# The low part of each weight slot, made by GpSimd in four operations of 512 columns in place of one of 2048

## What is computed

```python
def token_mix(x, pool_prev, mem_k, mem_v, pos0, w_in, b_in, ...):
    proj = x @ w_in + b_in                       # u, v, p, q, and three gates
    z = jax.nn.gelu(proj[..., :OFF_P])
    ...
    br_a = (u * mixed.reshape(N, L, A_WIDTH)) @ w_a_out
    p_ext = jnp.concatenate([pool_prev.astype(p.dtype), p], axis=1)
    br_b = pool_mix(p_ext, pos0, w_pool, ls_pool) @ w_b_out
    o = mem_attend(q..., mem_k.astype(q.dtype), mem_v.astype(q.dtype))
    br_m = o.reshape(N, L, MEM_WIDTH) @ w_m_out
    h = gates[:, :, 0] * br_a + gates[:, :, 1] * br_b + gates[:, :, 2] * br_m
    return h @ w_o, p_ext[:, -POOL_HIST:], v
...
y_p = layer_norm(DN_ALPHA * y_p + t_p, ln1_g[l], ln1_b[l])
f_p = moe_ffn(y_p.reshape(-1, D_MODEL), w_r[l], b_r[l], w1[l], b1[l], w2[l], b2[l])   # top 4 of 32 experts
y_p = layer_norm(DN_ALPHA * y_p + f_p, ln2_g[l], ln2_b[l])
```

## Time and profile before

| | |
|---|---|
| Time, median of 3 runs | 1342.45 us (1342.22 to 1343.2) |
| Time of the profiled execution | 1345.13 us |
| Its span, first to last instruction | 1343.3 us |
| TensorE busy (matmul) | 1278.1 us, 95% |
| VectorE busy | 421.4 us, 31% |
| ScalarE busy | 248.2 us, 18% |
| GpSimd busy | 222.4 us, 17%; of it L525: 39 operations, 183.5 us |
| Mean granted TensorE clock | 0.973 of full |
| The chain that ended last | TensorE 75%, DMA 16%, VectorE 4%, ScalarE 2%, GpSimd 1% |

### The profile page before, as it was taken

The page is one execution under the profiler, slowest core; times in us unless marked ns, Lnnn a source line. Parts: engine busy times, 40 slices in busy tenths (PEclk is TensorE's granted clock), DMA queues, the critical chain, the costliest instruction groups (busy, mean ns, idle before and its releaser), DMA issues.

```text
span 1343.3 us, 15957 instructions
## 1 busy us (share of the span) xinstructions
PE 1278.1 (95%) x6440; PEld 663.3 (49%) x6440; DVE 421.4 (31%) x783; ACT 248.2 (18%) x360; POOL 222.4 (17%) x99
## 2 busy tenths in 40 slices
PE   7999999998979999999999999999999999999994
PEld 7989889998843333333333333333333333333331
DVE  3670482284631313212222221312222131222225
ACT  3424443333230111101101010110101011010111
POOL 5536167665420000000000000000000000000001
PEclk9979999998959999999999999999999999999997
DMA  9534675741569999999999999999999999999991
GB/s 315 183 105 164 216 236 179 217 145 44 195 260 429 428 428 429 427 429 427 429 429 429 427 429 428 428 428 428 429 429 428 428 428 427 429 428 428 429 401 40
DMA packets 77179, 464.82 MB, mean 346 GB/s; under 512 B 5553, under 2 KB 44005, under 8 KB 52464
## 3 DMA queue, kind: packets, MB, share of 16 engines
q1 hardware_dynamic: 75616, 459.18, 83.5%
q0 software_dynamic: 1456, 5.11, 1.2%
q10 hardware_dynamic: 72, 0.03, 0.0%
HBM read 461.51 MB, written 2.90 MB: 346 GB/s over the span
## 4 chain that ended last, share of the span: by engine, by line
PE 75%; DMA 16%; DVE 4%; ACT 2%; issue 1%; POOL 1%; SPq 0%; ACTq 0%; DVEq 0%; POOLq 0%
PE ps L1619 27%; DMA big<-in_w 16%; PE ps L1298 15%; PE ps L1662 12%; PE ps L1592 6%; PE ps L1280 4%; PE ps L1309 2%; PE ps L1573 2%; PE ps L1644 1%; PE ps L1391 1%; ACT actT L775 1%; PE ps L1400 1%; POOL ring_lo L525 1%; PE ps L1377 1%; DVE hT_lo L1071 1%
## 5 line engine op out<-in xcount | busy, mean ns | idle before, releaser
L1619 PE MATMUL ps<-big,xg 128*64 128x512 f32 x2048 | 464.4, 597 | 11.4 <-DMA big<-in_w 11.1
L1619 PEld LDWEIGHTS ps<-big,xg 128*64 128x64 f32 x2048 | 139.9, 137 | 301.6 <-issue 264.1
L525 POOL TENSOR_TENSOR ring_lo<-ring,w_hi 128x2048 fp32r<-128x2048 f32 x39 | 183.5, 4708 | 125.2 <-ACT w_hi L606 125.1
L1662 PE MATMUL ps<-big,actT 128*64 128x512 f32 x768 | 171.9, 596 | 3.9
L571 POOL TENSOR_TENSOR yacc<-yacc,ln 128x512 f32<-128x512 f32 x2 | 3.3, 1642 | 949.8 <-ACT yacc L628 949.8
L770 ACT ACTIVATE sg<-gm 128x512 f32<-128x512 f32 x32 | 20.2, 631 | 541.5 <-DVE gm L1202 541.5
L1202 DVE TENSOR_SCALAR gm<-ps 128x512 f32<-128x512 f32 x32 | 22.1, 692 | 312.6 <-PE ps L1619 312.6
L1181 DVE TENSOR_TENSOR yacc<-ps,yacc 128x512 f32<-128x512 f32 (+1 forms) x90 | 61.9, 687 | 144.6 <-PE ps L1592 143.2
L1662 PEld LDWEIGHTS ps<-big,actT 128*64 128x64 f32 x768 | 52.3, 137 | 110.7 <-issue 91.4
L1174 DVE COPY ypair<-ps 64x512 f32<-64x512 f32 x32 | 22.2, 694 | 253.9 <-PE ps L1662 253.9
L1592 PE MATMUL ps<-ypair,pickT 128*128 128x512 f32 (+1 forms) x180 | 96.5, 631 | 0.0
(11 more groups left out here) (276 smaller groups left out, 1155.4 us busy)
## 6 DMA issues: line engine op xcount, KB each, us to landing
big<-in_w SPq DMA_DIRECT2D x176, 2048.0 KB, 22.3
spare<-in_w SPq DMA_DIRECT2D x16, 2048.0 KB, 23.8
ring<-in_w_in SPq DMA_DIRECT2D x24, 1024.0 KB, 6.4
ring<-in_cache_mem_k SPq DMA_DIRECT2D x4, 1024.0 KB, 5.0
ring<-in_cache_mem_v SPq DMA_DIRECT2D x4, 1024.0 KB, 6.6
ring<-in_w_a_out SPq DMA_DIRECT2D x4, 1024.0 KB, 9.8
ring<-in_w_o SPq DMA_DIRECT2D x4, 1024.0 KB, 4.8
ring<-in_w_mk SPq DMA_DIRECT2D x2, 1024.0 KB, 5.1
```

Source lines behind the costliest of these rows:

```text
L525: pool.tensor_tensor(ring_lo[:, SLOTS[key] % HR, :], slot(*key), w_hi[:, SPLITS.index(key) % 2, :].bitcast(F32), ALU.subtract)\
L1619: ins = pe.matmul(ps[CAP * hh:CAP * hh + CAP, b, :], xg[:, k, par, :], big[:, w1_big, SLOT * kk + 512 * p:SLOT * kk + 512 * p + 512], star ...
L1662: ins = pe.matmul(ps[CAP * dh:CAP * dh + CAP, YB, :], actT[:, kk, j, :], w[:, kk, 512 * dh:512 * dh + 512], start=False, stop=(j == 1 and ...
```

## The change

GpSimd's `lows` loops over four quarters of 512 columns. Each quarter is the same subtract on the same buffers; the semaphore `w_low` is raised by the last of the four only. Everything else is as it was, L532 too.

```diff
                 for key in keys:
                     pool.wait_ge(w_high, SPLITS.index(key) + 1)
-                    pool.tensor_tensor(ring_lo[:, SLOTS[key] % HR, :], slot(*key),
-                                       w_hi[:, SPLITS.index(key) % 2, :].bitcast(F32), ALU.subtract)\
-                        .then_inc(w_low, 1)
+                    for c in range(0, SLOT, SLOT // 4):
+                        part = slice(c, c + SLOT // 4)
+                        ins = pool.tensor_tensor(ring_lo[:, SLOTS[key] % HR, part], slot(*key)[:, part],
+                                                 w_hi[:, SPLITS.index(key) % 2, part].bitcast(F32), ALU.subtract)
+                    ins.then_inc(w_low, 1)
```

## The result

The changed kernel takes 1346.69 us (median) where the kernel before, run beside it, takes 1344.35. The ratio is 1.0021 with a 95% interval from 1.0014 to 1.0028: slower by 1.9 to 3.8 us. The interval lies on both sides of the 0.2% which I had set as the bound between "no change" and "slower"; the forecast was +1.7 us, and the result lies inside its range. The forecast of 1344.2 stood on the 1342.45 of three runs; the kernel before has a median of 1344.35 over 14 runs here, so the time is 2.5 us above the forecast, while the distance between the two medians, 2.3, is 0.6 more than forecast. The profiled execution of the changed kernel took 1345.54 us, its span is 1343.7.

What follows compares the result with a forecast made beforehand. Experts' weights set the pace from 395 us, so TensorE's gains or losses before that reach the end. 0.75 + 2.20 + 0.43 - 0.75 - 0.9 = +1.73 us on the 1342.45 median gives 1344.2; range 1340.5 to 1347.5.

Steps and rivals of the forecast that it cites:

- the port: While a GpSimd operation runs, VectorE operations with all inputs in SBUF stand still to its end, as if sharing a port.
- gA0: Slot on TensorE's path, wanted at 179.53 us: ready 0.75 us later with VectorE's turns; ends 0 and 1.2.
- wa0: Slot right behind gA0: four VectorE sums fall into it, ready at 189.61, a new stall of 2.20 us; ends 0 and 2.6.
- mv0: Slot with the tightest low part, 0.40 us to spare at 107.33, said to cover slots of up to 5.04 us.
- hT: TensorE's wait for hT at 322 to 325 us: blocked VectorE operations get turns, 0.9 us gained; ends 0 and 1.5.
- Who gets the port: Between two pieces, a VectorE operation that has waited a while gets its turn, so it waits for one piece, not four.
- the first rival: The port isn't given up between pieces; only slot growth counts, 0.3 to 1.6 us, 1342.8 to 1344.1; chance 0.17.
- The price of a piece: Each 512-column GpSimd subtract takes 1.18 us, so an undisturbed slot takes 4.72 in place of 4.64.
- rival two: TensorE's clock falls to its lower level at wa0's new stall, price 2.8 us at most, 1347.0; chance 0.20.
- gM1 and wm0: Two slots from 280.23 us, where VectorE's casts and subtracts get turns: second slot 0.43 us late; ends 0 and 1.1.
- gM3: Slot where TensorE waits 0.94 us at 309.59: earlier VectorE operations bring back 0.75; ends 0 and 0.94.
- rival three: Clock no longer falls at hT: 2.8 us back, 1341.4, or 1339.2 with wa0's stall spared too; chance 0.13.

Runs made afterwards that it cites:

- e2: Only slots gA0 and wa0 in four pieces, all others whole as in the kernel before; ratio to before 1.0023.
- e4: Kernel before with only one slot in four pieces, the first of wo, beside which hT's low part is made; ratio to before 0.9971.
- e10: The kernel of e4 run once more; 1341.15 us against 1344.61 for the kernel before, ratio 0.9970.
- e1: Changed kernel with slots gA0 and wa0 left whole, all others in four pieces; ratio to the kernel before 0.9996.
- e8: Changed kernel with GpSimd's two transfers of pout issued two slots later; 1348.84 us in one execution.
- e6: Kernel before with only the four slots of wo split, in eight pieces each; ratio to before 1.0013.
- e7: Kernel before with only the four slots of wo split, in two pieces each; ratio to before 0.9991.
- e9: Kernel before with only the first slot of wo split, in eight pieces; 1340.99 us against 1344.61, ratio 0.9974.
- e3: Changed kernel, but VectorE's chain of copies and sums waits until wa0 is made; ratio to the kernel before 1.0012.
- e5: Changed kernel with the four slots beside VectorE's chain of sums left whole, gA0 and wa0 among them; ratio to the kernel before 1.0000.

## Why the prediction was right, and where it wasn't

**What bounds the kernel, and the port.** Right: the stage of the experts keeps its length within 2.2 us, whenever it begins, and what moves is mainly in the places named. e2 puts the whole cost at gA0 and wa0, e4 and e10 put the gain at wo0. Two places weren't named: mv0, and wo1 where the clock stays up at hT (e1, e8).

**Who gets the port.** Right in the main: L1024's row was the rule, and the pieces of e6 and e7 show it at other sizes. L1124, the row that spoke for the first rival, again loses its turn in the changed kernel (started at 380.71, 2.61 us, 0.16 ahead of the third of three GpSimd operations end to end). That repeats the row; it doesn't show that the operation came too late, as I had taken it, and e9 speaks against that. VectorE's L1087 there, and GpSimd's piece behind it, from the timeline:

```profile
317.61 0.51 DVE L1087 TENSOR_TENSOR hT<-hT,gbuf 128x320 f32<-128x320 f32 x1
...
317.74 0.98 POOL L528 TENSOR_TENSOR ring_lo<-ring,w_hi 128x256 fp32r<-128x256 f32 x1
```

It starts 0.13 ahead of the boundary and has its turn at once. What kept L1124 out stays open, as with L1043 in the changed kernel. The Trainium skill, "GPSIMD Engine Reference", section "Instruction dispatch", had spoken for that rival too: each core goes on to its next instruction with nothing that joins them between two. These traces speak against drawing that from it: VectorE got in between pieces that were queued end to end, as at 317.74.

**The price of a piece.** Mis-sized: I took 1.18, near the quarter of the same operation, and it is 1.26 from start to start (5.06 for four), the upper end, which L572 had shown. It would have made my sum 1345.9. An undisturbed slot of 5.06 is also just over the 5.04 up to which mv0's 0.40 was to cover it: mv0 costs 0.2.

**gA0.** 0.75 forecast, 0.99 measured, of which 0.1 is mv0's. e3, where nothing of VectorE's chain stands in gA0, has 0.4 of it from the pieces alone.

**wa0.** The low part was to be ready at 189.61; TensorE got it at 189.73. Two errors cancel in that: its pieces cost 0.34 more, and the turns of the sums 4.3 us in place of 4.64. The stall was to be 2.20 and is 0.52, and the clock, which rival two had falling at wa0, fell one slot sooner, after gA0's wait of 2.11. By my own forecast gA0's wait was to grow from 1.20 to 1.95, but I asked only at wa0 whether the clock would fall. It made nearly no difference: eight matmuls at 2.02 and 1.86 in place of 1.17 are 1.5 us, with the edges 1.7, and TensorE comes to wa0 that much later, where it had to wait for 2.2 anyway. 0.52 and 1.70 are 2.22, my 2.20. Rival two had the place wrong: behind wa0's stall the lower clock would have come on top, ahead of it its price is taken up by the stall.

**gM1 and wm0.** 0.43 forecast, 0.58 measured, but at the other slot: gM1 was to be ready just in time and wm0 late. TensorE waits at gM1 (0.23, at 290.92) and not at wm0. gM1's pieces cost 0.34 more than reckoned, and two subtracts and a cast had their turns in it where I had one subtract and two casts. e5 has 0.6 at the same place.

**gM3.** This step failed: 0.75 was to come back and 0.02 was lost. L1086 ends 2.1 us sooner after its start (1.50 for 3.58), not 2.6: of the half microsecond that is missing, 0.2 is the length of the two pieces ahead of its turn; the rest is time that my 297.3 left out, of L1086 itself behind the boundary (0.4) or of the first piece, which VectorE holds up (1.54 us). The next two operations that meet a piece take 1.58 and 1.07 in place of 0.48 and 0.49, 1.7 more together, about as reckoned. That leaves 0.4, and the slot behind them is 0.42 longer, not 0.1. So the price of a piece, and a smaller term left out, turned 0.75 into nothing.

**hT.** 0.9 forecast, 1.11 measured. Another 1.11 came from the clock being low for a shorter time: a part of the 2.8 of rival three, which had a chance of 0.13. I had treated that as yes or no; the traces of e4 and e10 show that the same waits may bring a fall or none. That may also be why the times of the kernel before spread (1341.69 to 1346.85); with one trace of it this isn't shown.

**The sum.** +1.73 forecast, +1.59 in the two traces, because gM3 (0.77 missing) and the clock at hT (1.11 found) nearly cancel. That the sum came out so close is luck in these two terms. The times say 1.9 to 3.8, a little more than the traces; one execution of each doesn't hold the spread of the clock at hT, nor the wait at wo1 that comes where it stays up (e1, e8), and the cause of that difference stays open. The chances, 0.57 for no change and 0.35 for slower, lay on both sides of a result that stands at the bound itself.

## What to carry to other kernels

Splitting an operation that shuts another engine out doesn't free anything: it lets the other engine in at the boundaries, and that engine's work is added to the split operation. Ask for each place which of the two engines TensorE waits for: split only where it waits for the one that is shut out (here one slot of 39: 3.5 us gained), and leave whole what TensorE itself waits for. And when a chain is kept off one slot, look where it lands next.

## What the runs showed of the hardware

- A GpSimd subtract of fp32 costs about 0.14 us for each further instruction that it is split into: 4.64, 4.76, 5.06 and 5.63 us for 2048 columns in one, two, four and eight.
- A VectorE operation that was shut out got in at the next boundary between two GpSimd operations even where these were queued end to end (4.93, 2.71, 1.59 and 1.03 us beside one, two, four and eight pieces), and GpSimd then waited for the whole of it, so that one piece of the changed kernel took 3.33 us. Not every one did: L1126 (2.61 us), started 0.16 ahead of a boundary, missed it, though L1087 in e9, started 0.13 ahead of one, had its turn; and L1043, started while GpSimd issued transfers, missed four (6.20 us, against 1.41 in e8). Why is open.
- After TensorE waits of 2.11 and 2.12 us (after, e2), with full work on both sides, the granted clock went to 0.50; after 1.20 and 1.21 (before, e1) it stayed at 1.00. In e3 it stayed after 1.62 and went to 0.50 after 1.80. After the waits for hT of some 2.5 us together (1.60 and 0.95) it fell in one execution of a kernel (e4) and not in another (e10).
